# Attention two's scores from rounded high and low parts of queries and keys

## Chip, cores and metric

One core of one Trainium2 chip runs the whole program. The metric is device time in microseconds (us) from launch to end, the median of the runs taken. Lower is better.

## What is computed

Two transformer blocks run one after the other on 256 tokens of width 2048: a first one (attention, convolution, feed-forward) and a second one of two layers. The change lies in the first layer of the second block, whose attention ("attention two") has 16 query heads in four groups of four. Heads 0 to 7 (dense) see the 256 tokens and 256 context tokens; heads 8 to 15 (windowed) see a band of the tokens, the context and a sink. Cut to what matters:

```
q = h @ w_in[:, :Q_W]                       # 16 heads of 128
k, v of 2 + 2 groups, 256 tokens + 256 context tokens
s = q @ k.T * HEAD_DIM ** -0.5              # 256 x 512 for each head, float32
s = s + band                                # heads 8 to 15 only
p = softmax(s)                              # with the sink for heads 8 to 15
y = (p @ v) * silu(z)                       # z = h @ w_in[:, Q_W + KV_W:]
x = x + gate * rmsnorm(y @ w_out)
```

## The kernel before

All weight products are made exact enough by splitting each operand in two fp32r parts: a rounded high part and the rest, the low part, and adding three products (high by high, high by low, low by high). Weights come by DMA into `raw`; ScalarE (ACT) rounds each step of 128x1024 into `w_hi` (`split_hi`, L548), VectorE (DVE) subtracts and writes `w_lo` (`split_lo`, L1144), and TensorE (PE) multiplies (`step_tokens`, L2109 to L2111; `step_feature`, L2055 to L2057). There are four step slots, so ACT rounds step s + 4 when PE has finished step s. Each engine works its own instruction list in a written order, tied to the others by semaphores; nothing reorders it.

Attention two comes after the blocks `evq` and `evkv`, which make queries, keys and values; `evkv` also reads the context's features in `b_hi` and `b_lo`. PE transposes queries and keys; ACT copies them from PSUM in fp32 to `q_T` and `k_T` (`q_out`, L916). The attention itself lies inside the four blocks `evz` of the gate product. The function `head_slots` exists once on each engine, and a slot j of group i is one head h = 4i + j:

- PE: two fp32 score products 128x128 by 128x512 (L2431), the first transposes of head h - 1's probabilities (`prob_transposes`, L2406), a step of z, the second transposes, another step of z, and the products of head h - 1 with v (`weigh_v`, L2415).
- DVE: adds the band (L1844, windowed heads), reduces to the maximum (L1846), scales it (L1849 or L1852), waits for the exponentials, scales the probabilities (L1864), then `split_lo` (L1144), a modulation step (`mod_step`, L1184), `split_lo`, `mod_step`. In slot 1 of a group it also gates the group before (L1829), in slot 3 it makes that group's low parts (`z_split`, L1833).
- ACT: copies the product of head h - 2 and the first transposes of h - 1, waits for the maximum, takes the exponentials (L1008, and L1012 for the sink), then `split_hi`, copies the second transposes (`prob_copy`, L977), `split_hi`.
- GpSimd (POOL): `stage_q` copies the next head's queries to one of two buffers `q_stage2` (L520), once a group it copies the values (L527), and it issues the modulation weights' DMAs (L482), which wait for DVE.

## Time and profile before

| | us |
|---|---|
| median of 3 runs | 1823.88 (1823.8 to 1824.35) |
| profiled execution, its span (first to last instruction) | 1822.8 |
| PE busy in it | 1803.1 |
| DVE busy | 1468.4 |
| ACT busy | 902.7 |
| POOL busy | 112.4 |

The attention's slots run from 1262.6 to 1422.3 us of the span, 16 slots of about 10 us. The profile gives the span alone; the median of the runs is 1.1 us above it.

### The profile page before, as it was taken

The numbers are of one execution on the slowest core, as the hardware profiler recorded it, in microseconds if no ns is written. First come the engines' busy times: TensorE is split into PE (matmuls) and PEld (weight loads), VectorE is DVE, ScalarE is ACT, GpSimd is POOL, SyncE is SP. The second block draws the span as 40 slices with busy tenths as digits, with TensorE's granted clock in tenths as the row PEclk, the third lists the DMA queues.
The fourth block names the chain that finished last, engine by engine and source line by source line (L and its number), as shares of the span: only waits on it lengthen the run. The fifth ranks groups of instructions, "written<-read, shape, count | busy, mean of one in ns | idle before, by whom it ended". The sixth has DMA issues, their size and how long they took to land.

```text
span 1822.8 us, 26157 instructions
## 1 busy us (share of the span) xinstructions
PE 1803.1 (99%) x9898; PEld 1560.7 (86%) x9898; DVE 1468.4 (81%) x1704; ACT 902.7 (50%) x1176; POOL 112.4 (6%) x217
## 2 busy tenths in 40 slices
PE   8999999999999999999999999999999999999998
PEld 7899988888888888888888888888888888888986
DVE  6899998878888897889887788755788778897854
ACT  6444566555335533553354557423656545445453
POOL 0000000000000000000000000001111010001000
PEclk9999999999999999999999999999999999999999
DMA  9756448777786787778977865654665784878562
GB/s 326 256 175 199 153 157 301 263 242 256 265 289 226 264 292 231 247 260 287 248 255 270 313 213 163 230 184 149 221 211 203 273 294 137 277 242 282 191 227 97
DMA packets 191017, 426.93 MB, mean 234 GB/s; under 512 B 12480, under 2 KB 12864, under 8 KB 189760
## 3 DMA queue, kind: packets, MB, share of 16 engines
q1 hardware_dynamic: 158560, 323.74, 52.3%
q0 software_dynamic: 27648, 100.68, 16.6%
q10 hardware_dynamic: 4704, 1.07, 0.3%
q8 instruction: 73, 1.20, 0.3%
q14 instruction: 32, 0.26, 0.0%
HBM read 421.23 MB, written 4.21 MB: 233 GB/s over the span
## 4 chain that ended last, share of the span: by engine, by line
PE 94%; DVE 3%; ACT 1%; issue 1%; DMA 1%; DVEq 0%; POOLq 0%; ACTq 0%
PE banks L2064 23%; PE banks L2109 14%; PE banks L2110 14%; PE banks L2111 14%; PE banks L2070 12%; PE banks L2055 4%; PE banks L2057 4%; PE banks L2056 4%; PE banks L2415 2%; PE banks L2431 2%; PE banks L2172 1%; PE banks L2406 1%; ACT w_hi L548 0%; DVE w_lo L1144 0%; DMA mod_raw<-in_ev_mod_w 0%
## 5 line engine op out<-in xcount | busy, mean ns | idle before, releaser
L548 ACT ACTIVATE w_hi<-raw 128x1024 fp32r<-128x1024 f32 x552 | 579.5, 1058 | 659.3 <-PE banks L2111 334.6
L1144 DVE TENSOR_TENSOR w_lo<-raw,w_hi 128x1024 fp32r<-128x1024 f32 x552 | 666.9, 1222 | 242.5 <-ACT w_hi L548 240.5
L2064 PE MATMUL banks<-a_pair,w_hi 128*128 128x512 f32 x1792 | 431.2, 391 | 1.6 <-DVE a_pair L1246 0.9
L2064 PEld LDWEIGHTS banks<-a_pair,w_hi 128*128 128x128 f32 x1792 | 328.3, 188 | 65.3 <-issue 2.2
L2109 PE MATMUL banks<-w_hi,b_hi 128*128 128x512 f32 x808 | 316.2, 391 | 0.2 <-DVE b_lo L1409 0.2
L2111 PE MATMUL banks<-w_hi,b_lo 128*128 128x512 f32 x808 | 314.5, 389 | 0.0
L2110 PE MATMUL banks<-w_lo,b_hi 128*128 128x512 f32 x808 | 314.4, 389 | 0.0
L1184 DVE SCALAR_TENSOR_TENSOR mod_sum<-mod_raw,silu_c,mod_sum 128x1024 f32<-128x1024 f32 x240 | 302.9, 1283 | 11.3 <-DMA mod_raw<-in_ev_mod_w 7.6
L2070 PEld LDWEIGHTS banks<-a_pair,w_lo 128*128 128x128 f32 x1792 | 230.2, 191 | 8.7
L2070 PE MATMUL banks<-a_pair,w_lo 128*128 128x256 f32 x1792 | 234.6, 283 | 0.0
L2109 PEld LDWEIGHTS banks<-w_hi,b_hi 128*128 128x128 f32 x808 | 151.7, 188 | 31.9 <-DVE b_lo L1409 0.6
L2111 PEld LDWEIGHTS banks<-w_hi,b_lo 128*128 128x128 f32 x808 | 151.6, 188 | 31.8
L2110 PEld LDWEIGHTS banks<-w_lo,b_hi 128*128 128x128 f32 x808 | 151.7, 188 | 31.2
L2109 PE MATMUL banks<-w_hi,a_pair 128*128 128x512 f32 x376 | 148.6, 395 | 0.9 <-DVE a_pair L1274 0.8
L2055 PE MATMUL banks<-a_pair,w_hi 128*128 128x256 f32 x512 | 148.4, 290 | 0.0
L2110 PE MATMUL banks<-w_lo,a_pair 128*128 128x512 f32 x376 | 146.4, 389 | 0.0
L2111 PE MATMUL banks<-w_hi,a_pair 128*128 128x512 f32 x376 | 146.4, 389 | 0.0
L2057 PE MATMUL banks<-a_pair,w_lo 128*128 128x256 f32 x512 | 144.8, 283 | 0.0
L2056 PE MATMUL banks<-a_pair,w_hi 128*128 128x256 f32 x512 | 144.8, 283 | 0.0
L1352 DVE SCALAR_TENSOR_TENSOR mod_sum<-scratch,cols,mod_sum 128x256 f32<-128x256 f32 x240 | 98.9, 479 | 0.0
L2055 PEld LDWEIGHTS banks<-a_pair,w_hi 128*128 128x128 f32 x512 | 98.1, 192 | 0.4 <-ACT scratch L966 0.3
L2056 PEld LDWEIGHTS banks<-a_pair,w_hi 128*128 128x128 f32 x512 | 98.2, 192 | 0.3 <-issue 0.2
(246 smaller groups left out, 1680.7 us busy)
## 6 DMA issues: line engine op xcount, KB each, us to landing
raw<-in_w_ff SPq DMA_DIRECT2D x128, 1024.0 KB, 6.6
mod_raw<-in_ev_mod_w POOLq DMA_DIRECT2D x96, 512.0 KB, 5.4
mod_raw<-in_od_mod_w POOLq DMA_DIRECT2D x96, 512.0 KB, 5.3
raw<-in_ev_w_in SPq DMA_DIRECT2D x40, 1024.0 KB, 5.2
raw<-in_w_in SPq DMA_DIRECT2D x39, 1024.0 KB, 5.2
raw<-in_od_w_in SPq DMA_DIRECT2D x32, 1024.0 KB, 5.8
raw<-in_w_out SPq DMA_DIRECT2D x16, 1024.0 KB, 6.3
raw<-in_ev_w_out SPq DMA_DIRECT2D x16, 1024.0 KB, 6.7
```

The source lines that it names most:

```text
L548: nc.scalar.activation(w_hi[:, s % SLOTS], raw[:, s // 2, KPS * (s % 2):KPS * (s % 2) + KPS, :], ACT.Copy).then_inc(hi_ready, 1)
L1144: nc.vector.tensor_tensor(w_lo[:, s % SLOTS], raw[:, s // 2, KPS * (s % 2):KPS * (s % 2) + KPS, :], w_hi[:, s % SLOTS].bitcast(F32), ALU.s ...
L1184: nc.vector.scalar_tensor_tensor(s, mod_raw[:, half, :], c, s, ALU.mult, ALU.add).then_inc(mod_acc, 1)
L1352: e = nc.vector.scalar_tensor_tensor(y, src, w, y, ALU.mult, ALU.add)
L2055: nc.tensor.matmul(o, wh, hi[:, k, :], start=first and t == 0 and f % 2 == 0, stop=False, skip_group_check=True)
L2056: nc.tensor.matmul(o, wh, lo[:, k, :], start=False, stop=False, skip_group_check=True)
L2057: last = nc.tensor.matmul(o, wl, hi[:, k, :], start=False, stop=t == KPS - 1, skip_group_check=True)
L2064: e = nc.tensor.matmul(out[:, f, :], w_hi[:, s % SLOTS, t, P * f:P * (f + 1)], rows[:, :, KPS * s + t, :], start=s == 0 and t == 0, stop=F ...
L2070: e = nc.tensor.matmul(out[:, f, T:2 * T], w_lo[:, s % SLOTS, t, P * f:P * (f + 1)], rows[:, 0, KPS * s + t, :], start=False, stop=s == ST ...
L2109: nc.tensor.matmul(o, ah, w_hi[:, slot, t, :], start=s == 0 and t == 0, stop=False, skip_group_check=True)
L2110: nc.tensor.matmul(o, ah, w_lo[:, slot, t, :], start=False, stop=False, skip_group_check=True)
L2111: last = nc.tensor.matmul(o, lo[:, k, P * tt:P * (tt + 1)], w_hi[:, slot, t, :], skip_group_check=True, start=False, stop=s == STEPS - 1 a ...
```

## The change

The fp32 score products, two a head, become six fp32r products: high query by high key, high query by low key, low query by high key. The high parts are rounded by ACT: keys where they were copied before (`q_out`, two instructions in place of one), queries in a new instruction a head (`round_q`). The low parts of the keys are subtracted by DVE (`keys_low`, twice), those of the queries by GpSimd (`stage_q`), where it copied. All four kinds live in `b_hi` and `b_lo`, the tiles of the context features, so `round_q(0, 0)` waits until the last step of `evkv` is done. The loops of ACT over groups 2 and 3 and of PE over groups 1 to 3 are written out. `q_stage2` and `k_T` go.

```diff
-        k_T = view(R1, 4, 512)
+        k_hi = [b_hi[:, 4 * i + 2:4 * i + 4, :] for i in range(4)]
+        k_lo = [b_lo[:, 4 * i + 2:4 * i + 4, :] for i in range(4)]
...
-            def stage_q(h, par):
-                if not isinstance(h, int) or h >= 2:
-                    pool.wait_ge(scores, HEAD2 + h - 1)
-                nc.gpsimd.tensor_copy(q_stage2[:, par, :], q_T[:, span(h, 1), :].rearrange("p a t -> p (a t)")).then_inc(q_staged, 1)
+            def stage_q(h, tile):
+
+                pool.wait_ge(q_rounded, h + 1)
+                nc.gpsimd.tensor_tensor(b_lo[:, span(tile, 1), :], q_T[:, span(h, 1), :], b_hi[:, span(tile, 1), :].bitcast(F32),
+                                        ALU.subtract).then_inc(q_staged, 1)
...
+            def round_q(h, tile):
+
+                nc.scalar.activation(b_hi[:, span(tile, 1), :], q_T[:, span(h, 1), :], ACT.Copy).then_inc(q_rounded, 1)
...
                     e.then_inc(exp_done, 1)
+                    if j < 3 or not last:
+                        round_q(h + 1, 4 * i + (j + 1) % 2 if j < 3 else 4 * i + 4)
                     split_hi(ahead[0], [ahead[1]])
...
+            act.wait_ge(step_done, 4 + 8 * Z)
+            round_q(0, 0)
             head_slots(0, False, True)
             head_slots(1, False)
-            with act.Fori(2, 4) as i:
-                head_slots(i, True)
+            head_slots(2, True)
+            head_slots(3, True, last=True)
...
             each_ahead(BLOCK["evkv"] + 1, last_keys_beside)
 
+            def keys_low(m):
+
+                dve.wait_ge(q_T_ready, 5 + m)
+                src = aux[:, 0:2, :] if m == 0 else acc[1][:, :].rearrange("p (a n) -> p a n", a=2)
+                for a in range(2):
+                    e = nc.vector.tensor_tensor(k_lo[2 * m + a], src[:, a, :].rearrange("p (a t) -> p a t", a=2),
+                                                k_hi[2 * m + a].bitcast(F32), ALU.subtract)
+                e.then_inc(k_low, 1)
+
+            keys_low(0)
...
+                    if first and j == 2:
+                        keys_low(1)
                     split_lo(ahead[0], [ahead[1]])
...
-                    if first and j in (1, 3):
+                    if first and j in (0, 3):
+                        pe.wait_ge(k_low, 1 + j // 3)
+                    if first and j == 1:
                         pe.wait_ge(acc_free, 2 + ACC["evz"])
-                        pe.wait_ge(q_T_ready, 6 if j == 3 else 5)
                     pe.wait_ge(q_staged, h + 1)
                     for tt in range(TT):
-                        e = nc.tensor.matmul(score2[j % 2][:, 512 * tt:512 * (tt + 1)], q_stage2[:, j % 2, P * tt:P * (tt + 1)],
-                                             k_T[:, span(i, 1), :].rearrange("p a t -> p (a t)"), start=True, stop=True)
+                        out = score2[j % 2][:, 512 * tt:512 * (tt + 1)]
+                        qh = b_hi[:, 4 * i + j % 2, P * tt:P * (tt + 1)]
+                        nc.tensor.matmul(out, qh, k_hi[i].rearrange("p a t -> p (a t)"), start=True, stop=False)
+                        nc.tensor.matmul(out, qh, k_lo[i].rearrange("p a t -> p (a t)"), start=False, stop=False)
+                        e = nc.tensor.matmul(out, b_lo[:, 4 * i + j % 2, P * tt:P * (tt + 1)], k_hi[i].rearrange("p a t -> p (a t)"),
+                                             start=False, stop=True)
                     e.then_inc(scores, 1)
```

How the instructions stand. The names are the program's tensors; `banks` is PSUM, `scratch` holds `q_T` among others, and a row's line number is that of its own kernel. First PE, at the end of `evkv` and the first head's scores, before:

```order
L2110 MATMUL banks<-w_lo,b_hi 128x512
L2111 MATMUL banks<-w_hi,b_lo 128x512
L2431 MATMUL banks<-scratch 128x512 [waits q_staged,q_T_ready]
L2431 MATMUL banks<-scratch 128x512
L2055 MATMUL banks<-a_pair,w_hi 128x256 [waits split_done,acc_free]
L2056 MATMUL banks<-a_pair,w_hi 128x256
```

and PE in the same place now:

```order
L2139 MATMUL banks<-w_hi,b_lo 128x512
L2462 MATMUL banks<-b_hi 128x512 [waits q_staged,k_low,q_T_ready]
L2463 MATMUL banks<-b_lo,b_hi 128x512
L2464 MATMUL banks<-b_hi,b_lo 128x512
L2462 MATMUL banks<-b_hi 128x512
L2463 MATMUL banks<-b_lo,b_hi 128x512
L2464 MATMUL banks<-b_hi,b_lo 128x512
L2083 MATMUL banks<-a_pair,w_hi 128x256 [waits split_done,acc_free]
```

The two score products have become six, and the first of them waits for `k_low` as well as for the staged query. Next ACT, from its last step of `evkv` to the first head's exponentials, before:

```order
L965 ACTIVATE scratch<-banks 128x512 [waits step_done]
L966 ACTIVATE scratch<-banks 128x2x256
L548 ACTIVATE w_hi<-raw 128x1024 [waits step_done]
L965 ACTIVATE scratch<-banks 128x512
L966 ACTIVATE scratch<-banks 128x2x256
L1008 ACTIVATE mod_sum,soft<-banks,soft 128x512 [waits neg_max]
```

and ACT in the same place now:

```order
L976 ACTIVATE scratch<-banks 128x512 [waits step_done]
L977 ACTIVATE scratch<-banks 128x2x256
L551 ACTIVATE w_hi<-raw 128x1024 [waits step_done]
L976 ACTIVATE scratch<-banks 128x512
L977 ACTIVATE scratch<-banks 128x2x256
L928 ACTIVATE b_hi<-scratch 128x256 [waits step_done]
L1019 ACTIVATE mod_sum,soft<-banks,soft 128x512 [waits neg_max]
L1019 ACTIVATE mod_sum,soft<-banks,soft 128x512
L928 ACTIVATE b_hi<-scratch 128x256
```

The rounding of head 0's query (L928) stands behind five instructions that themselves wait for the end of `evkv`. Last ACT in the second slot of a windowed group, before:

```order
L977 ACTIVATE scratch<-banks 128x512 [waits prob_tr]
L1008 ACTIVATE mod_sum,soft<-banks,soft 128x512 [waits neg_max]
L1008 ACTIVATE mod_sum,soft<-banks,soft 128x512
L1012 ISA
L1012 ACTIVATE soft<-soft,cols 128x2
L545 REGISTER_ALU
L548 ACTIVATE w_hi<-raw 128x1024 [waits raw_in3,step_done]
L976 REGISTER_ALU
L977 ACTIVATE scratch<-banks 128x512 [waits prob_tr]
```

and ACT in the same place now:

```order
L988 ACTIVATE scratch<-banks 128x512 [waits prob_tr]
L1019 ACTIVATE mod_sum,soft<-banks,soft 128x512 [waits neg_max]
L1019 ACTIVATE mod_sum,soft<-banks,soft 128x512
L1023 ACTIVATE soft<-soft,cols 128x2
L928 ACTIVATE b_hi<-scratch 128x256
L551 ACTIVATE w_hi<-raw 128x1024 [waits raw_in3,step_done]
L988 ACTIVATE scratch<-banks 128x512 [waits prob_tr]
```

The new rounding stands between the exponentials and the two instructions behind them, a weight rounding and the copy of head h - 1's second transposes.

## Rows read from the trace of the kernel before

**Rows 1.** The page: span, busy time by engine, chain that ended last.

```profile
span 1822.8 us, 26157 instructions
...
PE 1803.1 (99%) x9898; PEld 1560.7 (86%) x9898; DVE 1468.4 (81%) x1704; ACT 902.7 (50%) x1176; POOL 112.4 (6%) x217
...
PE 94%; DVE 3%; ACT 1%; issue 1%; DMA 1%; DVEq 0%; POOLq 0%; ACTq 0%
```

**Rows 2.** Timeline of PE, heads 10 to 15: start, duration, engine, line, operands, count.

```profile
1380.04 1.89 PE L2415 MATMUL banks<-scratch 128*128 128x256 f32 x8
...
1400.36 2.00 PE L2415 MATMUL banks<-scratch 128*128 128x256 f32 x8
1402.19 1.88 PE L2431 MATMUL banks<-scratch 128*128 x4
1403.91 0.60 PE L2406 MATMUL banks<-ident,mod_sum 128*128 128x128 f32 x4
```

**Rows 3.** Timeline of PE where `evkv` ends and head 0 begins.

```profile
1262.37 0.39 PE L2111 MATMUL banks<-w_hi,b_lo 128*128 128x512 f32 x1
1262.60 1.88 PE L2431 MATMUL banks<-scratch 128*128 128x512 f32 x4
```

**Rows 4.** Timeline of ACT in the same place.

```profile
1262.79 0.60 ACT L965 ACTIVATE scratch<-banks 128x512 f32<-128x512 f32 x1 [4.38 <-PE banks L2111]
...
1265.19 0.61 ACT L966 ACTIVATE scratch<-banks 128x512 f32<-128x512 f32 x1
```

**Rows 5.** Timeline of DVE in the same place.

```profile
1264.86 1.23 DVE L1144 TENSOR_TENSOR w_lo<-raw,w_hi 128x1024 fp32r<-128x1024 f32 x1 [4.05 <-ACT w_hi L548]
```

**Rows 6.** Groups by line and shape, ACT: count, busy us, mean ns, idle before.

```profile
L736 ACT ACTIVATE b_hi<-table 128x256 fp32r<-128x256 f32 x8 | 3.3, 418 | 0.3
```

**Rows 7.** Busy time by stretch at the end: us, engines, PEclk, DMA, GB/s.

```profile
1814.00:1816.00 2.00, 0.29 (x2) 0.00 (x0) 1.99 (x4) 0.98 (x3) 0.00 (x0) 1.00 0.54 200
1816.00:1818.00 2.00, 0.00 (x0) 0.00 (x0) 1.94 (x4) 0.00 (x0) 0.00 (x0) 0.66 0.62 214
```

**Rows 8.** Timeline of PE at the program's start.

```profile
6.03 5.51 PE L2178 MATMUL banks<-ones 128*128 128x128 f32 x26 [6.03 <-DMA scratch<-in_x]
```

**Rows 9.** Who waited for whom, PE: us in total, times, longest.

```profile
PE banks L2172 <- DVE ln_rstd L1238: 1.8, 2, 1.2
```

**Rows 10.** Timeline of DVE, heads 6 and 7.

```profile
1323.24 1.22 DVE L1846 TENSOR_REDUCE soft<-banks 128x2 f32<-128x1024 f32 x1
...
1330.95 1.23 DVE L1144 TENSOR_TENSOR w_lo<-raw,w_hi 128x1024 fp32r<-128x1024 f32 x1 [0.89 <-ACT w_hi L548]
...
1333.31 1.23 DVE L1846 TENSOR_REDUCE soft<-banks 128x2 f32<-128x1024 f32 x1
```

**Rows 11.** Timeline of DVE, heads 8 to 15.

```profile
1343.53 0.69 DVE L1844 TENSOR_TENSOR banks<-banks,table 128x512 f32<-128x512 f32 x1
...
1394.88 0.69 DVE L1844 TENSOR_TENSOR banks<-banks,table 128x512 f32<-128x512 f32 x1
...
1404.76 0.69 DVE L1844 TENSOR_TENSOR banks<-banks,table 128x512 f32<-128x512 f32 x1
...
1414.63 0.69 DVE L1844 TENSOR_TENSOR banks<-banks,table 128x512 f32<-128x512 f32 x1
```

**Rows 12.** Timeline of ACT, head 13.

```profile
1397.24 0.69 ACT L1008 ACTIVATE mod_sum<-banks,soft 128x512 f32<-128x512 f32 x1 [2.33 <-DVE soft L1849]
...
1399.71 0.59 ACT L977 ACTIVATE scratch<-banks 128x512 f32<-128x512 f32 x1
```

**Rows 13.** Groups by line and shape, POOL.

```profile
L520 POOL COPY scratch<-scratch 128x256 f32 x12 | 4.9, 410 | 0.1
```

**Rows 14.** Timeline of POOL, head 5, the copy of the values.

```profile
1311.59 0.92 POOL L527 COPY scratch<-scratch 128x512 f32 x1 [6.85 <-PE banks L2415]
```

**Rows 15.** Timeline of DVE, heads 4 and 5.

```profile
1309.05 1.28 DVE L1184 SCALAR_TENSOR_TENSOR mod_sum<-mod_raw,silu_c,mod_sum 128x1024 f32<-128x1024 f32 x1
...
1311.95 1.63 DVE L1184 SCALAR_TENSOR_TENSOR mod_sum<-mod_raw,silu_c,mod_sum 128x1024 f32<-128x1024 f32 x1
```

More of the change, by code:

```diff
@@ L224, in build_program @@
         prob_T2 = view(R2, 4, T)
-        q_stage2 = view(R2 + 1024, 2, T)
         v_stage2 = view(R2 + 1536, 4, HD)
@@ L301, in build_program @@
         v_staged = sem("v_staged")
+        q_rounded = sem("q_rounded")
+        k_low = sem("k_low")
         scores = sem("scores")
@@ L515, in _ @@
             load_mod("od_shift", "od", 0, 1, KT)
-            def stage_q(h, par):
-                if not isinstance(h, int) or h >= 2:
-                    pool.wait_ge(scores, HEAD2 + h - 1)
-                nc.gpsimd.tensor_copy(q_stage2[:, par, :], q_T[:, span(h, 1), :].rearrange("p a t -> p (a t)")).then_inc(q_staged, 1)
+            def stage_q(h, tile):
+                pool.wait_ge(q_rounded, h + 1)
+                nc.gpsimd.tensor_tensor(b_lo[:, span(tile, 1), :], q_T[:, span(h, 1), :], b_hi[:, span(tile, 1), :].bitcast(F32),
+                                        ALU.subtract).then_inc(q_staged, 1)
             def head_slots(i, slots):
                 for j in slots:
-                    stage_q(4 * i + j + 1, (j + 1) % 2)
+                    stage_q(4 * i + j + 1, 4 * i + (j + 1) % 2 if j < 3 else 4 * i + 4)
                     if j == 0:
@@ L913, in q_out @@
                 act.wait_ge(q_tr, n + 1)
-                src = acc[1][:, :].rearrange("p (a n) -> p a n", a=2) if n == 5 else aux[:, 0:2, :]
-                dst = (q_T[:, FT * n:FT * (n + 1), :] if n < 4 else k_T[:, 2 * (n - 4):2 * (n - 4) + 2, :])
-                nc.scalar.activation(dst, src if n >= 4 else src.rearrange("p a (h t) -> p (a h) t", t=T),
-                                     ACT.Copy).then_inc(q_T_ready, 1)
+                if n < 4:
+                    nc.scalar.activation(q_T[:, FT * n:FT * (n + 1), :], aux[:, 0:2, :].rearrange("p a (h t) -> p (a h) t", t=T),
+                                         ACT.Copy).then_inc(q_T_ready, 1)
+                else:
+                    src = acc[1][:, :].rearrange("p (a n) -> p a n", a=2) if n == 5 else aux[:, 0:2, :]
+                    for a in range(2):
+                        e = nc.scalar.activation(k_hi[2 * n - 8 + a], src[:, a, :].rearrange("p (a t) -> p a t", a=2), ACT.Copy)
+                    e.then_inc(q_T_ready, 1)
+            def round_q(h, tile):
+                nc.scalar.activation(b_hi[:, span(tile, 1), :], q_T[:, span(h, 1), :], ACT.Copy).then_inc(q_rounded, 1)
             b = BLOCK["evq"]
@@ L993, in z_round, with head_slots @@
                 nc.scalar.activation(b_hi[:, span(4 * i, FT), :], q_T[:, span(4 * i, FT), :], ACT.Copy).then_inc(z_hi, 1)
-            def head_slots(i, windowed, first=False):
+            def head_slots(i, windowed, first=False, last=False):
                 for j in range(4):
@@ L1816, in _ @@
             each_ahead(BLOCK["evkv"] + 1, last_keys_beside)
+            def keys_low(m):
+                dve.wait_ge(q_T_ready, 5 + m)
+                src = aux[:, 0:2, :] if m == 0 else acc[1][:, :].rearrange("p (a n) -> p a n", a=2)
+                for a in range(2):
+                    e = nc.vector.tensor_tensor(k_lo[2 * m + a], src[:, a, :].rearrange("p (a t) -> p a t", a=2),
+                                                k_hi[2 * m + a].bitcast(F32), ALU.subtract)
+                e.then_inc(k_low, 1)
+            keys_low(0)
             def late_rope():
@@ L2448, in _ @@
             head_slots(0, True)
-            with pe.Fori(1, 4) as i:
+            for i in range(1, 4):
                 head_slots(i)
```

## The prediction

> **What bounds the kernel now.** I read the page first: PE is busy 1803.1 of 1822.8 us and is 94% of the chain that ended last [rows 1]. So what PE saves or waits inside the span counts one to one. Then I read PE's timeline in the attention slots. A head's scores (L2431, four records, two for each fp32 product) begin at 1402.19 and the transposes behind them at 1403.91: 1.72 us [rows 2]. PE never shows idle time there, because the ends of matmuls are modelled; the waits have to be looked for in durations. The products with v (L2415, eight records) take 1.89 us in head 11's slot (1380.04) and 2.00 in head 13's (1400.36) [rows 2]. That is a wait of 0.11. It ends when ACT finishes the copy L977, 1399.71 + 0.59 = 1400.30 [rows 12]. And that copy comes late because DVE began the head late: its band addition at 1394.88 [rows 11]. So in the windowed heads DVE and ACT together run at PE's pace already. The eight heads took DVE from 1343.53 to 1414.63, 71.1 us for seven slots, 10.16 a slot [rows 11]. PE needs 10.07: in the dense heads, where DVE starts right behind the scores, a slot goes from 1323.24 to 1333.31 [rows 10], that is 1.72 for the scores and 8.35 for all else.
>
> **The change on PE.** The fp32r products of 128x512 start 0.23 us apart (L2111 at 1262.37, the next at 1262.60) [rows 3]. Six of them cost 6 x 0.227 = 1.36 us, so a head saves 0.36 us and 16 heads 5.7. PE's own slot becomes 9.71. That is the whole gain.
>
> **The start of head 0.** Before, the first scores began at 1262.60, at once behind `evkv` [rows 3], since their query had been staged and their keys copied long before. Now two chains have to end first, and both start when `evkv` ends.
> - Query: ACT's five instructions behind `evkv` begin at 1262.79, the fifth at 1265.19 and lasts 0.61 [rows 4]; instructions of ACT overlap by some 0.1, so the rounding starts near 1265.7. It takes 0.42, the time of a 128x256 fp32r rounding [rows 6]: 1266.1. Then GpSimd subtracts. No row shows a subtraction there. Its copy of the same size takes 0.41 [rows 13]; that is the lower bound, since it reads one operand fewer, and I take 0.8, twice that, as the upper: 1266.5 to 1267.0.
> - Keys: `keys_low(0)` stands behind the last `split_lo` of that stretch, which starts at 1264.86 and occupies DVE for 1.14 (the next instruction starts before its 1.23 are over) [rows 5]: 1266.0. Two operations on 128x512 from PSUM, 0.69 each as in L1844 [rows 11], overlapping by 0.1: ready at 1267.3.
>
> The keys end last. Scores start at 1267.4, end at 1268.8 instead of 1264.3: **+4.4 us**, head 0's saving included. What is queued behind on PE is all of the z product, for which nothing else is late. Between 4.1 (some overlap more) and 5.5 (GpSimd's subtraction over 1 us) is the range.
>
> **The clock.** PE stands still for 4.7 us, from 1262.7. In the trace PE's last matmul ends at 1814.3, and the granted clock is 0.66 over 1816 to 1818, so it fell from the upper level (2.4 GHz) to half of it (1.2 GHz) near 1816.6, 2.4 us after the last work [rows 7]. PE's longest wait of another kind after the start is 1.2 us [rows 9], so the trace has no case of its own. I expect the fall here too. At the program's start, 26 matmuls of 128x128 took from 6.03 to 11.4, 0.21 us apart [rows 8]; at the upper level four records of that shape take 0.60 altogether, starts some 0.11 apart [rows 2]. So about 5 us of work at half pace before the clock rose. Half of 5 us is 2.5 lost; if the rise comes sooner, 1.7. I take **+2.0**, with 0 and 2.5 as ends.
>
> **Dense heads.** ACT's rounding and GpSimd's subtraction lie beside PE's z steps: in head 6's slot DVE still waits 0.89 for ACT, and ACT for PE, before L1144 at 1330.95 [rows 10]. So heads 1 to 8 start their scores earlier by 8 x 0.36: **-2.9**. But DVE enters head 8 later than now. The `split_lo` at 1330.95 is tied to the end of a z step, that is to where the slot began, not to where it ends; a slot shorter by 0.36 leaves DVE 0.36 behind. Head 7's slot then has the `z_split` L1833 as well: 1333.31 to 1343.53 is 10.22 us [rows 10, 11], 0.5 over the new 9.71; with GpSimd's collision (below, 0.35) DVE is 1.2 behind the scores at head 8, where it is only 0.1 to 0.2 behind now.
>
> **Windowed heads.** Here is the main point. Two chains close the loop on DVE. DVE's own work from one band addition to the next takes 9.87 in head 14's slot (1404.76 to 1414.63), with nothing for PE to release in it; it waits only for the exponentials of its own scores. The slots with the value copy and the `z_split` take longer: the seven sum to 71.1 [rows 11]. None of this becomes shorter with shorter scores. The second chain holds PE to DVE: `weigh_v` waits for L977, which in head 13 ends 1400.30 - 1394.88 = 5.4 after the band addition [rows 11, 12]. PE's natural time from the end of the scores to that place is 8.35 less the 1.72 of the products with v (1402.19 - 1400.36 - 0.11) [rows 2]: 6.6. So DVE may start at most 1.2 behind the scores' end before PE waits, and with the new rounding ahead of L977 (0.33 of ACT, 0.42 less the overlap) at most 0.9. At head 8 it is 1.2 behind. From there on PE runs at DVE's pace. Now the `weigh_v` of head 15's slot begins 7 x 10.07 + 6.6 + 0.3 (waits of the kind seen in head 13's slot, in two or three slots) = 77.4 after the end of head 8's scores. Then it begins 1.2 + 71.1 + 5.8 (5.4 and the latency, with 0.33 of rounding) = 78.1 after it. That is **+0.7** where PE's own arithmetic would say -2.5.
>
> **The collision.** GpSimd's subtraction starts when ACT's rounding is done, about 0.4 after the exponentials, just where DVE scales the probabilities (L1864) and then runs L1144. In the trace a GpSimd copy beside DVE's work costs DVE time: L1184 takes 1.63 at 1311.95 beside the value copy of 1311.59, where the same takes 1.28 at 1309.05 [rows 14, 15]. So +0.35. The subtraction reads twice as much as the query copy, and the copy in the old slots lay beside PSUM work mostly. I take 0.35 a slot; the lower bound is 0.1 (the weight rounding on ACT comes 0.33 later, of which 0.28 were free), the upper 0.7. In the windowed loop it counts fully: 7 x 0.35 = **+2.5** (0.7 to 4.9).
>
> The Trainium skill speaks against this change more strongly. Its page "SBUF — State Buffer" ("Who interferes with whom") says that a DVE instruction with two SBUF inputs contends with a GpSimd instruction that reads SBUF, and that the second to issue fully blocks. By that rule DVE would stand for the rest of the GpSimd instruction; the trace agrees that it stands, for 0.35 of the copy's 0.92 us. Its page "GPSIMD Engine Reference" (3.1) gives 4497 ns for an addition of 2048 elements a partition; an estimate from it for 256 elements is 0.56 us, and with full blocking the term would be 7 x 0.56 = 3.9 in place of 2.5, the total 1.4 higher.
>
> **Other edits, at nothing.** `keys_low(1)` (1.3 us of DVE in head 2's slot) and the split copy of the keys lie where DVE and ACT have over 3 us until PE's next need; were that gone they would cost 1.3 once. The written-out loops replace branches whose slots already start 10.07 apart like the rest. GpSimd's first two modulation DMAs move behind the first subtraction, by 5 us; head 0's `mod_step` moves by 4 as well.
>
> **Sum.** +4.4 + 2.0 - 2.9 + 0.7 + 2.5 = +6.7 on a span of 1822.8, that is 1829.5; the median of the runs lies 1.1 above the profiled span, so 1830.6. 0.2% (3.65 us) is what a measurement of this kernel can tell from no change: above 1827.5 it is slower.
>
> **Rivals.**
> - The clock does not fall: +4.7, 1828.6. For it: the only fall seen is at the end, and 4.7 us is only twice that delay. Chance 0.2.
> - The slots do run at PE's pace, because DVE has more room than I think (its slots shrink with PE's). Then +4.4 + 2.0 - 5.4 = +1.0: 1824.9, no change. For it: the heads 0 to 7 have such room; against: 9.87 in head 14. Chance 0.2.
> - Faster: the wait at head 0 is not there, since all PE's saving stays. -5.7: 1818.2. It decides at a wait below 2 us (with no fall of the clock and PE's pace kept). Against: the order of DVE and ACT behind `evkv`. Chance 0.05.
> - GpSimd blocks DVE twice a slot or stretches to over 1 us, 0.8 or more a slot: 7 x 0.8 = 5.6 in place of 2.5, and 0.5 more at head 8: 1834.2. Chance 0.05.
> - The forecast: 0.5.
>
> Slower by over 0.2%: 0.5 + 0.05 + most of 0.2, less the lower end of the forecast: 0.69. Within: 0.24. Faster: 0.07. The lower end leaves out the faster case, the upper the last one: 1824.0 to 1834.0.
>
> **What the profile after will show.** PE's first scores near 1267.4, idle before them with DVE's `keys_low` as releaser; a granted clock below 1 in the following microseconds; six score records in 1.36 to 1.5 us; L988's copy ending just as `weigh_v` starts in heads 8 to 15, and band additions 10.2 to 10.6 apart; GpSimd's subtraction at 0.5 to 0.8 us and DVE's L1864 or L1144 longer by 0.2 to 0.5. I am wrong if the slots run 9.7 apart up to the end, or if the clock stays at 1.

## The result, and the profile after

The changed kernel takes 1832.41 us (median of 4 runs, 1831.68 to 1832.7), the kernel before 1823.9 (4 runs, 1823.8 to 1824.35). The ratio is 1.0045, with a 95% interval of 1.0033 to 1.0057: slower, by 8.5 us. The profiled execution of the changed kernel spans 1830.0 us. Three executions, one of the kernel before and two in the experiments, ran at a mean granted clock of 0.65 to 0.77 and took 2191 to 2574 us; medians and ranges here leave them out.

The page of the changed kernel answers to [rows 1]:

```profile
span 1830.0 us, 26114 instructions
...
PE 1801.1 (98%) x9930; PEld 1568.0 (86%) x9930; DVE 1476.8 (81%) x1708; ACT 906.5 (50%) x1194; POOL 118.4 (6%) x217
...
PE 94%; DVE 3%; ACT 1%; issue 1%; DMA 0%; DVEq 0%; SPq 0%; ACTq 0%
```

PE is busy 2.0 us less than before and the span is 7.2 longer, so PE now waits. In the list of who waited for whom, two lines on PE are new (engine, tile and line, what released it, us in total, times, longest):

```profile
PE banks L2462 <- DVE b_lo L1838: 4.6, 1, 4.6
PE banks L2443 <- issue: 4.3, 6, 1.5
```

The first is head 0's scores behind `keys_low`. PE's timeline has it, and what comes after it:

```profile
1266.84 0.77 PE L2462 MATMUL banks<-b_hi 128*128 128x512 f32 x1 [4.62 <-DVE b_lo L1838]
1267.40 0.63 PE L2463 MATMUL banks<-b_lo,b_hi 128*128 128x512 f32 x1
1267.83 0.63 PE L2464 MATMUL banks<-b_hi,b_lo 128*128 128x512 f32 x1
...
1276.29 0.40 PE L2462 MATMUL banks<-b_hi 128*128 128x512 f32 x1
1276.52 0.40 PE L2463 MATMUL banks<-b_lo,b_hi 128*128 128x512 f32 x1
```

Head 0's products start 0.43 apart, head 1's 0.23. The busy time by stretch shows why (us from and to; length; PE, PEld, DVE, ACT, POOL; PEclk, the granted clock, third from the right):

```profile
1262.00:1264.00 2.00, 0.22 (x1) 0.00 (x0) 0.00 (x0) 1.75 (x3) 0.00 (x0) 1.00 0.00 0
1264.00:1266.00 2.00, 0.00 (x0) 0.00 (x0) 1.69 (x2) 1.56 (x4) 0.29 (x1) 0.75 0.00 0
1266.00:1268.00 2.00, 1.16 (x3) 1.00 (x4) 0.74 (x2) 0.00 (x0) 1.48 (x3) 0.50 0.53 94
1268.00:1270.00 2.00, 2.00 (x8) 1.61 (x7) 0.22 (x1) 0.00 (x0) 0.00 (x0) 0.50 1.04 402
1270.00:1272.00 2.00, 2.00 (x12) 2.00 (x12) 1.97 (x4) 0.76 (x3) 0.00 (x0) 0.54 1.03 417
1272.00:1274.00 2.00, 2.00 (x19) 2.00 (x18) 1.93 (x5) 1.39 (x5) 0.76 (x2) 1.00 0.39 152
```

PE stopped at 1262.2. The clock was at 1 up to 1264, 0.75 over the next 2 us (so it halved at 1265.0), 0.50 up to 1270 and 0.54 over the last 2 us of them (back near 1271.8). PE worked from 1266.84 to 1271.8 of it, 5.0 us at 1.2 GHz: 2.5 lost.

The second new line is the products with v. Around this wait in head 9's slot the timelines of DVE, POOL, ACT and PE have these rows, in this order:

```profile
1363.16 1.36 DVE L1890 TENSOR_SCALAR mod_sum<-mod_sum,soft 128x512 f32<-128x512 f32 x2
...
1363.31 0.92 POOL L522 TENSOR_TENSOR b_lo<-scratch,b_hi  x1 [3.30 <-ACT b_hi L928]
...
1363.88 0.58 ACT L988 ACTIVATE scratch<-banks 128x512 f32<-128x512 f32 x1
...
1364.57 0.67 PE L2443 MATMUL banks<-scratch 128*128 128x256 f32 x2 [0.79 <-issue]
```

PE starts 0.11 after ACT's copy has ended (1363.88 + 0.58 = 1364.46); in [rows 2, 12] it was 0.06. But now it has stood idle for 0.79. The copy is late because DVE was late: ACT's exponentials of this head had waited 2.88 us for DVE's scaled maximum. What makes DVE's loop longer is beside it in the first two rows: GpSimd's subtraction lies beside the scaling of the probabilities (L1890, L1864 before), and the pair of scalings takes 1.36. Behind the last head nothing is subtracted, and there the same pair takes 0.88:

```profile
1347.94 0.69 DVE L1870 TENSOR_TENSOR banks<-banks,table 128x512 f32<-128x512 f32 x1
...
1422.49 0.69 DVE L1870 TENSOR_TENSOR banks<-banks,table 128x512 f32<-128x512 f32 x1
...
1426.90 0.88 DVE L1890 TENSOR_SCALAR mod_sum<-mod_sum,soft 128x512 f32<-128x512 f32 x2
```

The first two of these rows are the band additions of heads 8 and 15: 74.55 us for seven slots, where [rows 11] give 71.10. The trace also has the two scalings of a pair apart. Here is line L1890 in head 9's slot (duration in ns: shortest, median, longest), and then DVE and GpSimd in head 12's slot:

```profile
L1890 DVE TENSOR_SCALAR mod_sum<-mod_sum,soft x2: 491/724/957, 1363.2 to 1363.6; 128x512 f32<-128x512 f32 x2
...
1395.39 1.36 DVE L1890 TENSOR_SCALAR mod_sum<-mod_sum,soft 128x512 f32<-128x512 f32 x2
...
1395.35 0.72 POOL L522 TENSOR_TENSOR b_lo<-scratch,b_hi 128x256 fp32r<-128x256 f32 x1 [3.13 <-ACT b_hi L928]
```

In head 9 the first scaling starts before the subtraction and takes 0.49, what it takes alone; the second starts behind the subtraction's start, takes 0.96 and ends 0.29 after it (1363.56 + 0.96 = 1364.52 against 1364.23). In heads 12 to 14 the subtraction starts 0.04 before the first scaling. Read alone, the first scaling there takes 0.97 and the second 0.47. In both orders one of the two scalings stands, and the pair grows by 0.48.

To see where the 7.2 us of the span arose I compare the starts of the products with v (L2415, now L2443) of heads 0, 7 and 15, in PE's timeline. First before, then after:

```profile
1278.40 0.84 PE L2415 MATMUL banks<-scratch 128*128 128x256 f32 x3
...
1349.82 0.38 PE L2415 MATMUL banks<-scratch 128*128 128x256 f32 x1
...
1428.76 1.46 PE L2415 MATMUL banks<-scratch 128*128 128x256 f32 x6
```

```profile
1284.30 1.03 PE L2443 MATMUL banks<-scratch 128*128 128x256 f32 x4
...
1353.79 1.53 PE L2443 MATMUL banks<-scratch 128*128 128x256 f32 x6
...
1436.20 1.89 PE L2443 MATMUL banks<-scratch 128*128 128x256 f32 x8
```

| stretch | before | after | difference |
|---|---|---|---|
| start of the span to head 0's | 1278.40 | 1284.30 | +5.9 |
| head 0's to head 7's | 71.42 | 69.49 | -1.9 |
| head 7's to head 15's | 78.94 | 82.41 | +3.5 |
| head 15's to the end | 394.0 | 393.8 | -0.2 |

### The profile page after: what moved, and what is told of

Read it like the earlier page. It is cut to its first block, busy times and chain, and to the rows that moved or that the text cites. A ratio compares the mean times of both kernels' runs of the same rounds, so it can differ in the third digit from the quotient of the medians.

```text
span 1830.0 us, 26114 instructions
## 1 busy us (share of the span) xinstructions
PE 1801.1 (98%) x9930; PEld 1568.0 (86%) x9930; DVE 1476.8 (81%) x1708; ACT 906.5 (50%) x1194; POOL 118.4 (6%) x217
## 4 chain that ended last, share of the span: by engine, by line
PE 94%; DVE 3%; ACT 1%; issue 1%; DMA 0%; DVEq 0%; SPq 0%; ACTq 0%
PE banks L2092 22%; PE banks L2137 14%; PE banks L2138 14%; PE banks L2139 14%; PE banks L2098 12%; PE banks L2083 4%; PE banks L2084 4%; PE banks L2085 4%; PE banks L2443 2%; PE banks L2200 1%; PE banks L2434 1%; ACT w_hi L551 1%; DVE w_lo L1159 1%; PE banks L2462 0%; PE banks L2464 0%
## 5 line engine op out<-in xcount | busy, mean ns | idle before, releaser
L484 POOL DMA_DIRECT2D mod_raw<-in_ev_mod_w x90 | 47.5, 528 | 806.0 <-DVE mod_sum L1199 726.4
```

Of the source, the lines that this page charges most:

```text
L484: nc.gpsimd.dma_start(mod_raw[:, half, :], mod_w[layer][:, span(kt, 1), part * D + half * MH:part * D + (half + 1) * MH]).then_inc(mod_in[ ...
```

## The experiments

Each is an edit of the changed kernel where nothing else is said. Band additions stand for the pace of the windowed heads: the time from head 8's to head 15's, seven slots.

**Keeping PE at work while it waits.** 21 products of `ones` are put ahead of head 0's scores; their result is used nowhere.

```diff
+                    if first and j == 0:
+                        keep_warm(21)
                     if first and j in (0, 3):
                         pe.wait_ge(k_low, 1 + j // 3)
```

> The changed kernel, with 21 matmuls of 128x128 ones on PE ahead of head 0's scores, to fill the wait; their result is overwritten. Theory (the clock's fall costs 2.5 us by itself): the granted clock stays at 1, PE stands busy in place of idle, the scores still start when the keys' low parts are ready: 1832.4 - 2.5 = 1829.9. Rival (the fall costs nothing, because something else is late behind head 0 anyway): 1832.4.

Measured: 1829.35 (ratio 1.0028, 1.0017 to 1.0039), 3.1 less than the changed kernel. The granted clock is 1 all the time in which DVE, ACT and GpSimd are still at head 0's operands:

```profile
1264.00:1266.00 2.00, 2.00 (x20) 2.00 (x19) 1.73 (x2) 1.52 (x4) 0.33 (x1) 1.00 0.03 8
1266.00:1268.00 2.00, 2.00 (x14) 1.72 (x13) 0.70 (x2) 0.00 (x0) 1.45 (x3) 1.00 0.62 97
```

So the fall comes from PE's standing still. It costs 2.5 by the granted clock and 3.1 by the medians. The two profiled executions give less: their spans differ by 2.3 (1830.0 and 1827.7), and from head 0's scores to its product with v it is 15.23 (1266.75 to 1281.98) in place of 17.46 (1266.84 to 1284.30), 2.2 less. The windowed heads kept their pace (74.57).

**Head 0's operands made earlier.** `evkv` is two blocks of eight weight steps. ACT rounds head 0's query in the second of them, right behind the copy of the keys, instead of behind the end of `evkv` (in the trace at 1241.60 in place of 1265.12), and DVE makes the first keys' low parts there too (1249.37 in place of 1265.45). The wait for the last step of `evkv`, which the change put ahead of `round_q(0, 0)`, was not needed for this one tile: its last reader comes earlier in that block.

```diff
@@ ACT, the last block of evkv @@
                 if m == 1:
+                    round_q(0, 0)
...
-            act.wait_ge(step_done, 4 + 8 * Z)
-            round_q(0, 0)
@@ DVE, the last block of evkv @@
-            keys_low(0)
+            def keys_beside(i):
+                last_keys_beside(i)
+                if i == 4:
+                    keys_low(0)
```

> The changed kernel, with head 0's query rounded right after the keys' copy (its tile was last read four steps before) and the first two keys' low parts subtracted four weight steps earlier. Theory (wait at head 0 of 4.6 us and the clock's fall of 2.5 us): no wait of PE there, clock at 1, 1832.4 - 7.1 = 1825.3. Rival (DVE's loop bounds the dense heads too, so that an earlier start is lost in them): 1828 or more. Rival 2 (the windowed heads are the whole loss): 1832.4.

Measured: 1826.81 (ratio 1.0014, 1.0005 to 1.0024), 5.6 less than the changed kernel and not 7.1. The wait of 4.62 is gone, and the clock stays at 1. DVE's band addition in head 8 comes at 1342.70, 5.2 earlier than 1347.94, and the span is 5.3 shorter. So what is missing was lost ahead of the windowed heads. PE's timeline has it in two new waits, both before head 2's scores:

```profile
1269.85 0.47 PE L2464 MATMUL banks<-b_hi 128*128 128x512 f32 x1 [0.38 <-POOL b_lo L522]
...
1279.00 1.97 PE L2445 MATMUL banks<-scratch 128*128 128x256 f32 x8 [0.90 <-issue]
```

Head 1's scores wait 0.4 for GpSimd's subtraction of their query, and head 0's product with v waits 0.9 for ACT's copy of its transposes (1278.31 + 0.59 = 1278.90). From head 0's scores to its product with v it is 16.87 here and 15.23 in the last experiment, in which PE never stood idle ahead of them either. That is 1.6, about the 1.5 that are missing. So the expectation's first rival came true in part, in heads 0 and 1 alone. The windowed heads themselves are as slow as without the edit, 74.54:

```profile
1342.70 0.69 DVE L1872 TENSOR_TENSOR banks<-banks,table 128x512 f32<-128x512 f32 x1
...
1417.24 0.69 DVE L1872 TENSOR_TENSOR banks<-banks,table 128x512 f32<-128x512 f32 x1
```

**No subtraction on GpSimd.** The low part of the query isn't made; the third product reads what lies in its tile. PE waits for ACT's rounding (`q_rounded`) where it waited for the subtraction. Arguments left out here are marked `...`:

```diff
             def stage_q(h, tile):
-                pool.wait_ge(q_rounded, h + 1)
-                nc.gpsimd.tensor_tensor(b_lo[:, span(tile, 1), :], ..., ALU.subtract).then_inc(q_staged, 1)
+                return
```

> The changed kernel without GpSimd's 16 subtractions; the low part of each query is left out of the computation (the third product reads what the tile last held), all PE, DVE and ACT instructions stay. Theory (GpSimd's subtraction lengthens DVE's scaling of the probabilities from 0.88 to 1.37 us, and DVE sets the windowed heads' pace): band additions 10.16 apart in place of 10.65, 0.49 less behind at head 8, 1832.4 - 7 x 0.49 - 0.49 = 1828.5. Rival (ACT's rounding ahead of the weight rounding sets the pace): within 1 us of 1832.4.

Measured: 1828.44 (ratio 1.0025, 1.0015 to 1.0035), 4.0 less than the changed kernel, where 3.9 were expected. The groups by line have the scaling of the probabilities at 484 ns each, what it takes in the kernel before:

```profile
L1888 DVE TENSOR_SCALAR mod_sum<-mod_sum,soft 128x512 f32<-128x512 f32 x32 | 14.1, 484 | 0.6
```

and the band additions span 71.61 (1346.77 to 1418.38). So the subtraction is worth 74.55 - 71.61 = 2.9 us in the windowed heads, through DVE. The other 0.9 lies at head 0: the clock was low for 3.4 us only (1266.3 to 1269.7) in this execution, and from head 0's scores to its product with v it is 16.56 in place of 17.46. The expectation counted eight collisions and no clock, so that its total is met so closely is in part luck. ACT's rounding, its rival, is not free: 71.61 is 0.5 above [rows 11]. Without the collision the weight rounding, which now stands behind the query's, ends at 1361.29 + 1.05 = 1362.34 in head 9's slot, and DVE's `split_lo` starts at 1362.38, 0.85 behind the start of the scalings; before it was 0.80.

**The subtraction beside something else.** ACT rounds the next head's query ahead of its wait for the maximum, so GpSimd subtracts while DVE reads the scores from PSUM. All work is done.

```diff
+                    if j < 3 or not last:
+                        round_q(h + 1, 4 * i + (j + 1) % 2 if j < 3 else 4 * i + 4)
                     act.wait_ge(neg_max, HEAD2 + h + 1)
...
                     e.then_inc(exp_done, 1)
-                    if j < 3 or not last:
-                        round_q(h + 1, 4 * i + (j + 1) % 2 if j < 3 else 4 * i + 4)
```

> The changed kernel, with ACT's rounding of the next head's query moved from behind the exponentials to ahead of the wait for the maximum, where ACT idles 1.5 to 2.9 us; nothing left out. Theory: GpSimd's subtraction then lies beside DVE's band addition and maximum, which read PSUM, so DVE's scaling takes 0.88 again: 3.9 less, and 0.33 less of ACT ahead of the copy that PE waits for: 1828.2. Rival (the collision only moves to other DVE work, the weight subtractions or modulation steps): within 1 us of 1832.4.

Measured: 1829.30 (ratio 1.0028, 1.0017 to 1.004), 3.1 less than the changed kernel where the theory had 4.2. Its runs spread widely, from 1827.69 to 1831.16. In the windowed heads it does what it should: 71.32 (1348.78 to 1420.10), with the scaling at 484 ns. Some 0.7 of it was lost again in heads 0 to 3: head 3's product with v starts at 1315.29 where the changed kernel has 1314.60. A reason that the groups by line suggest, and that no run tested: the scaling of the maximum in the dense heads, two elements a partition, which took 169 ns in the changed kernel,

```profile
L1878 DVE TENSOR_SCALAR soft<-soft 128x2 f32<-128x2 f32 x8 | 5.9, 733 | 0.3
```

now takes 733 on average. The collision is moved off the windowed heads' loop, not ended; in that sense the rival came true in the dense heads.

**Both.** The early start of head 0 and the early rounding together.

> The early start of head 0 (query rounded and first keys' low parts made during the last step of evkv) together with the rounding placed ahead of ACT's wait for the maximum. Theory (the loss has two parts that add: the start of head 0 with the clock, and the collision of GpSimd's subtraction with the scaling of the probabilities): 1826.8 of the early start alone, less 3.2 for the seven windowed slots (74.5 to 71.3) = 1823.6, band additions 71.3 over seven slots, scaling 484 ns. Rival (the two overlap: with the early start the windowed heads are held by something else): band additions stay at 74 or more, 1826 to 1827. If nothing holds DVE and dense heads keep all their gain: down to 1821.

Measured: 1823.68 (11 runs, 1823.19 to 1824.75; ratio 0.9998, 0.9989 to 1.0007), band additions 71.48 (1342.77 to 1414.25). It fell as the sum said: the two edits gave 5.6 and 3.1 alone and 8.7 together. The two losses add, and without them the change is worth nothing: PE's 5.7 us are still not there. By the starts of PE's scores the seven slots from head 8 to head 15 take 71.5, where PE's own 7 x 9.74 would be 68.2; that is 3.3 of them. Another 1.3 go in head 1's slot (11.09, where the kernel before has 10.10 less the saving). In its rows the small operation's delay can be read to the end. DVE's timeline, then GpSimd's:

```profile
1314.52 0.81 DVE L1880 TENSOR_SCALAR soft<-soft 128x2 f32<-128x2 f32 x1
...
1314.55 0.75 POOL L522 TENSOR_TENSOR b_lo<-scratch,b_hi  x1
```

It ends at 1315.33, GpSimd's at 1315.30. The Trainium skill's page "SBUF — State Buffer" ("Who interferes with whom") says that `tensor_scalar` can take the port pair shared with GpSimd, and that the loser stands for the whole of the other's instruction; these two rows agree. It also says that whoever issues first has the pair; here the waiting DVE operation has the earlier start by 0.03, so a start in the record need not show who had it.

**One product in place of two, nothing added.** The kernel before, with a single fp32r product (rounded query by rounded keys) where a fp32 product was. The low parts are left out. `q_out` rounds the keys as it copies them, GpSimd copies the query to a tile of `b_hi`, and PE's loop over groups is written out.

```diff
-nc.tensor.matmul(score2[j % 2][...], q_stage2[:, j % 2, ...], k_T[:, span(i, 1), :]..., start=True, stop=True)
+nc.tensor.matmul(score2[j % 2][...], b_hi[:, 4 * i + j % 2, ...], k_hi[i]..., start=True, stop=True)
```

> The kernel before with one fp32r product of 128x512 where a fp32 product was (rounded query by rounded keys; the low parts are left out), so PE's scores take 0.45 us a head in place of 1.72 and no other engine has more work than before. Theory (windowed heads run at DVE's pace): dense heads gain up to 8 x 1.27 = 10.2, windowed heads nothing, band additions still 71 over seven slots: about 1814. Rival (windowed heads run at PE's pace): 16 x 1.27 = 20.3, slots 8.8 apart, 1803.6.

Measured: 1818.19 (ratio 0.9967, 0.9954 to 0.998). Of 20.3 us that PE saves, 5.8 arrive. DVE's timeline:

```profile
1319.59 1.23 DVE L1849 TENSOR_REDUCE soft<-banks 128x2 f32<-128x1024 f32 x1
...
1328.21 1.22 DVE L1849 TENSOR_REDUCE soft<-banks 128x2 f32<-128x1024 f32 x1
...
1337.94 0.70 DVE L1847 TENSOR_TENSOR banks<-banks,table 128x512 f32<-128x512 f32 x1
...
1409.01 0.70 DVE L1847 TENSOR_TENSOR banks<-banks,table 128x512 f32<-128x512 f32 x1
```

From head 8 to head 15 it is 71.07, where [rows 11] give 71.10, although each slot has 1.27 us less for PE. So DVE's loop over the windowed heads takes 71.1 whatever PE does. In the kernel before PE needs as much (7 x 10.07 = 70.5, and its scores of heads 8 to 15 start 70.8 apart), so both engines bind there, and nothing that PE saves can show. The theory missed on the dense heads (10.2 expected, 5.8 measured). By the starts of PE's scores the slots of heads 3 and 5 to 7 take 8.81, the whole saving. But the slots of heads 1, 4 and 8 take 10.46, 9.93 and 10.41, 1.6, 1.1 and 1.6 more than the kernel before less 1.27, because DVE has fallen behind by then. Head 7's slot shows how: with the `z_split` it takes 9.73 of DVE's own work (1328.21 to 1337.94), 0.3 under PE's old 10.07, while head 6's takes 8.62.

**The loops written out, nothing else.** The kernel before with ACT's loop over groups 2 and 3 and PE's over 1 to 3 written out.

```diff
-            with pe.Fori(1, 4) as i:
+            for i in range(1, 4):
                 head_slots(i)
```

> The kernel before with nothing changed but the two loops written out (ACT over groups 2 and 3, PE over groups 1 to 3). Theory: nothing, 1823.9, within 0.5. Rival (code loading or branches are part of the change's cost or gain): over 1 us away, either sign.

Measured: 1824.44 (ratio 1.0002, 0.9993 to 1.0012). No difference that can be told from none, as the theory said. The lines above are PE's loop; ACT's was written out in the same way.

**Taking work from DVE.** If DVE holds the windowed heads, relieving it should set PE's gain free. The kernel with both repairs, and with the scaling of the probabilities on ACT, behind the second weight rounding of the slot, and DVE's two scalings taken out:

```diff
                     split_hi(ahead[0], [ahead[1] + 1])
+                    act.wait_ge(inv_ready, HEAD2 + h + 1)
+                    for tt in range(TT):
+                        nc.scalar.activation(prob2[:, p, tt, :], prob2[:, p, tt, :], ACT.Copy,
+                                             scale=soft[:, p, tt:tt + 1]).then_inc(prob_ready, 1)
```

> The kernel with the early start of head 0 and the early rounding, and besides that the scaling of the probabilities taken from DVE and given to ACT, behind the second weight rounding of a slot, where ACT stands idle for 1 to 3 us. DVE's loop loses 0.8 us a slot: 71.3 for seven windowed slots become 65.7 of work, less than PE's 7 x 9.71 = 68.0. Theory (DVE's loop is what held back the gain of PE): slots run at PE's pace, band additions 68 over seven slots, 1823.9 less the 5.7 that six fp32r products save over two fp32 ones = 1818.2, up to 1819.5 with small waits at heads 0 to 2. Rival (ACT or GpSimd holds the slots once DVE doesn't): band additions 70 or more, 1822 to 1824.

The same on the kernel before:

> The kernel before (fp32 score products) with the same move of the scaling from DVE to ACT and nothing else. Theory: DVE was only just the bound of the windowed slots (71.1 for seven, PE's own 7 x 10.07 = 70.5), so -0.3 to -0.9, 1823.3. Rival (DVE's waits cost PE more than the durations show): 1822 or less. Its distance to the kernel above is what the change is worth where no engine but PE binds: 5.7 less what head 0 still waits, 4.5 to 5.7.

Measured: 1825.06 (ratio 1.0005, 0.9996 to 1.0014) and 1829.1 (ratio 1.0027, 1.0017 to 1.0037). Both theories missed. In the first the rival's sign is there (band additions 71.01), at 1 us above its range; in the second neither value came. The waits of PE in the first of the two:

```profile
PE banks L2085 <- ACT scratch L1001: 3.4, 3, 1.2
...
PE banks L2436 <- ACT mod_sum L1038: 1.6, 2, 1.0
```

and ACT and PE at one of them:

```profile
1340.43 1.32 ACT L1038 ACTIVATE mod_sum<-mod_sum,soft 128x512 f32<-128x512 f32 x2
1341.77 1.28 ACT L1001 ACT_TABLE_LOAD   x1
1343.07 1.02 ACT L1001 ACTIVATE scratch<-banks 128x1024 f32<-128x1024 f32 x1
...
1344.14 0.39 PE L2085 MATMUL banks<-a_pair,w_hi 128*128 128x256 f32 x1 [1.16 <-ACT scratch L1001]
```

The idle time that I had counted on ACT is there, but in slot 3 of a group what stands behind it is the read of the gate (L1001, `z_silu`), which frees the PSUM block for PE's next z step. The 1.3 us went on the path there. Three such waits are 3.4, the scaling in head 0 is 1.0 more. In the kernel before the same two lines are 2.8 and 1.3, 0.9 less than its 5.0. That is because the idle time is not the whole of a wait: the first record behind it is longer too (0.39 in the last row above, where 0.28 is usual). By starts nothing is missing: from head 0's scores to the last head's product with v it is 171.1 (1263.60 to 1434.68) where the kernel before has 166.2 (1262.60 to 1428.76), 4.9 more. Heads 1, 4, 8 and 12 take 0.9 to 1.2 more each, and the last head's product another 0.8.

**The same, only where nothing waits.** ACT scales in slots 0 to 2 except head 0's; DVE keeps the rest. Again on the kernel with both repairs, and on the kernel before.

```diff
-                    dve.wait_ge(inv_ready, HEAD2 + h + 1)
-                    for tt in range(TT):
+                    if j == 3 or first and j == 0:
+                        dve.wait_ge(inv_ready, HEAD2 + h + 1)
+                    for tt in range(TT if j == 3 or first and j == 0 else 0):
                         nc.vector.tensor_scalar(prob2[:, p, tt, :], ...)
```

> Early start of head 0, early rounding, and the scaling on ACT only in the slots where nothing of PE waits behind it there: slots 0 to 2 of a group, not the very first head; DVE keeps slot 3, where ACT has the gate's PSUM block to read next. The kernel with all scaling on ACT took 1825.06 and lost 3.4 us in three waits of PE for that read and 1.0 at head 0. Theory (those waits were the whole of what it lost): 1825.1 - 3.4 - 1.0 = 1820.7, slots 9.74 apart, faster than before by over 2 us. Rival (DVE, late by the z_split of slot 3, holds the next group): 1822 to 1823.7, no better than with the scaling left on DVE.

> The kernel before with the same move of the scaling for slots 0 to 2. With all of it on ACT it took 1829.1, waiting 2.8 for the gate's read and 1.3 for the scaling. Theory (PE's own pace with fp32 products is 10.07 a slot, and DVE held it by under 1 us in all): 1823.3. The distance to the kernel with six products is then 2.6 (theory) and at most 5.7 (PE bound everywhere). Rival: ACT's extra work is dear wherever it lies, 1825 or more.

Measured: 1822.53 (11 runs, 1821.41 to 1823.74; ratio 0.9993, 0.9984 to 1.0002) and 1824.37 (11 runs, 1824.22 to 1824.66; ratio 1.0002, 0.9993 to 1.0011). The first has the lowest median of all versions that do the whole work, 9.9 below the changed kernel and 1.4 below the kernel before; its interval doesn't exclude no change. The theory of the first, 1820.7, missed by 1.8; its rival (DVE, late by the `z_split` of slot 3) said 1822 to 1823.7 and came. The second lies between its theory, 1823.3, and its rival, 1825, and the interval can't tell it from the theory. Neither wait of the last experiment is left. DVE's band additions of heads 8, 11, 12 and 15:

```profile
1342.88 0.69 DVE L1877 TENSOR_TENSOR banks<-banks,table 128x512 f32<-128x512 f32 x1
...
1372.21 0.69 DVE L1877 TENSOR_TENSOR banks<-banks,table 128x512 f32<-128x512 f32 x1
...
1383.22 0.69 DVE L1877 TENSOR_TENSOR banks<-banks,table 128x512 f32<-128x512 f32 x1
...
1412.55 0.69 DVE L1877 TENSOR_TENSOR banks<-banks,table 128x512 f32<-128x512 f32 x1
```

The three slots without DVE's scaling are now 9.78 apart on average (10.02 for the first, with the copy of the values beside it, then 9.63 and 9.68), near PE's 9.74; head 11's, slot 3, still takes 11.01, since it keeps the scaling and has the `z_split`. All seven take 69.67. In the kernel before with the same move they take 70.47 (1343.20 to 1413.67), which is PE's 7 x 10.07. That gave PE nothing that shows in the time: its scores of heads 8 to 15 start 70.6 apart where they were 70.8. So of the 5.7 us that PE saves, 1.84 show where DVE is relieved in three slots of four (1824.37 - 1822.53); the runs of the two don't overlap. Of the rest, PE's longest wait is again ahead of head 0's product with v, 1.3 us.

## Why the prediction was right, and where its terms were off

The forecast was 1830.6, slower, and 1832.41 came, inside the range. Its own case, of five, is the one that happened: PE waits at head 0, the clock falls, and from head 8 on PE runs at DVE's pace, which GpSimd's subtraction makes longer.

- **The start of head 0** (+4.4). The keys were the last, as said; PE waited 4.62 for them, less the head's 0.36 that is 4.3. Scores began at 1266.84 and not 1267.4, because in this execution the whole program ahead ran 0.5 earlier (ACT's first row there is 0.54 before that of [rows 4]).
- **The clock** (+2.0, 0 to 2.5). It fell, and cost 2.5 by the record and 3.1 by the run in which PE was kept at work. By the two profiled executions it is 2.2. So the term was 0.2 to 1.1 too small. The rival without a fall (1828.6) is out.
- **Dense heads** (-2.9 for eight). The table has -1.9 for seven slots, so some -2.2. PE's slot came out at 9.74 (9.71 forecast), but two were longer, head 4's with 9.95 and the one from head 6's product with v to head 7's with 9.97; the term took it that none would be.
- **Windowed heads** (+0.7 and +2.5). The table has +3.5, where 3.2 was said. The collision is 2.9 by the kernel without the subtraction, 0.42 a slot, where 0.35 was taken. The lateness of DVE at head 8 was forecast as 1.2. I read 1.0 from the timelines: the transposes start at 1346.93, right behind the scores, the band addition at 1347.94. Before it is 0.34 by the same reading (1343.19 and 1343.53), not the 0.1 to 0.2 of the prediction.
- **The rival in which slots run at PE's pace** (1824.9) is out by two runs. With head 0's wait gone the windowed heads kept 74.54, and with PE's scores 1.27 shorter in the kernel before they kept 71.07.
- **The written-out loops** at nothing: right, +0.5 with an interval of -1.3 to +2.2. **GpSimd's subtraction**, 0.5 to 0.8: 0.73 alone, 0.85 where it meets DVE.
- **The sum.** The wait is 4.6, the clock 2.2, the rest up to head 0's product with v -0.6, the other two stretches -1.9 and +3.5: 7.8 in all. The span grew by 7.2 only, since `evkv` ended 0.4 earlier (1262.22 against 1262.60) and what follows head 15 was 0.2 shorter. So the terms were too low by about 1 us, and 0.6 of it was hidden by parts of the program that the change doesn't touch. That is luck, but a small one.
- **From span to median.** I took 1.1, from the kernel before. Each run lies some 1.6 above its own span, and the profiled execution of before was the slowest of its three (1824.35), that of after the fastest of its four (1831.68). So the span was 0.5 above the forecast (1829.5), and the other 1.3 of the 1.8 are the choice of 1.1 and of those executions.

On the full block of the Trainium skill's page "SBUF — State Buffer" ("Who interferes with whom"): I priced the collision by a row (0.35 of a copy) and gave the full block as 3.9. Measured are 2.9 for the seven slots. The rows agree with a full block, and still it costs less than the subtraction lasts. The small operation stands until GpSimd ends. Of the pair of scalings one runs through and the other stands (0.49 and 0.96 in head 9). The subtraction has 0.67 left when the second scaling starts at 1363.56, but that scaling ends 0.29 after it and not 0.49, so 0.2 of its own time pass while it stands, and 0.48 are lost.

What stays open: why the version with the early rounding alone spreads over 3.5 us, why the clock's fall is 3.1 by the medians and 2.2 in the traces, and whether head 1's slot could be relieved; its waits were read, and no run tested a cure.

## What to carry to other kernels

Before making the busiest engine faster, look at each stretch for a second engine whose loop is closed there. PE was busy 99% of the span, yet 1.27 us less a slot in the windowed heads left their pace as it was (71.07 against 71.10 for seven), because DVE's own work between two band additions was as long as PE's slot.

New operands for the first step of a stage need their own look. Steady slots had room for the rounding and the subtraction, but head 0 had none, and its wait cost the clock on top. Preparing them in the block before, where DVE and ACT stood idle, gave back 5.6 us of 8.5.

Idle time of an engine is room only if what stands behind it in program order can wait. ACT had 1 to 3 us idle in each slot and still could not take 1.3 us in the slot where its next instruction frees PE's bank.

## What the runs showed of the hardware

- PE stood still from 1262.2 and the granted clock went from 1 to half (1.2 GHz) at 1265.0; it came back to 2.4 GHz 6.8 us later in one execution of the changed kernel, and 3.4 us later in one of the kernel without the subtraction, which has the same wait (4.6 us). The stretch from head 0's scores to its product with v took 17.46 and 16.56: the same stall doesn't cost the same each time. In the version with the early start the clock had no fall.
- A DVE operation on two elements a partition, 0.17 us by itself, takes 0.81 when it starts 0.03 us ahead of a GpSimd subtraction of 128x256, and ends with it. The maximum, which reads PSUM, takes 1.22 beside the same subtraction (head 9 with both repairs, 1353.76, the subtraction from 1354.32) and 1.22 without it.
- A pair of DVE scalings of 128x512: 0.88 alone, 1.36 beside GpSimd's subtraction, whichever of the two starts first. One scaling keeps its 0.49, the other takes 0.96. The subtraction takes 0.72 where it starts first, and 0.92 where it starts 0.15 behind the first scaling.
